# Prompt attention moved between the value steps of layer 1, and four dot rows moved ahead of the query tiles

## The reference, cut to what matters

```python
qp, kp, vp = _qkv(hp, na_w_qkv[j], na_b_qkv[j])          # prompt: 128 tokens
op = _merge_heads(_context_attention(qp, kp, vp)) @ na_w_out[j] + na_b_out[j]
new_k_layers.append(kp); new_v_layers.append(vp)
qs, ks_, vs = _qkv(hs, na_w_qkv[j], na_b_qkv[j])         # sample: 256 tokens
att = _neighbourhood_attention(qs, ks_, vs, cache_k[:, j], cache_v[:, j], na_rpb[j])
os_ = _merge_heads(att) @ na_w_out[j] + na_b_out[j]
yp = _layer_norm(DEEPNORM_ALPHA * yp + gm_p * op, ln_g[i, 0], ln_b[i, 0])
```

## Time and profile before

| | |
|---|---|
| median of three executions | 1055.6 us |
| the profiled execution's own time | 1054.8 us |
| its span from first to last instruction | 1053.0 us |
| busy: PE, DVE, ACT, POOL | 983.7, 704.7, 184.1, 196.6 us |
| mean granted clock of PE | 0.970 |
| chain that ended last: PE, DVE, DMA, SP's queue | 72%, 9%, 9%, 6% |

### The profile page before, as it was taken

The page is one execution under the profiler, slowest core; times in us unless marked ns, Lnnn a source line. Parts: engine busy times, 40 slices in busy tenths (PEclk is TensorE's granted clock), DMA queues, the critical chain, the costliest instruction groups (busy, mean ns, idle before and its releaser), DMA issues.

```text
span 1053.0 us, 28184 instructions
## 1 busy us (share of the span) xinstructions
PE 983.7 (93%) x11412; PEld 585.2 (56%) x11412; DVE 704.7 (67%) x1782; ACT 184.1 (17%) x435; POOL 196.6 (19%) x304
## 2 busy tenths in 40 slices
PE   7999999999899999999899999899979999999872
PEld 2555555565556656566545554575445666666451
DVE  6458874955756666666667995685576666666457
ACT  4342223003210000000140010562231000000002
POOL 1400000610132222222110000354013222222112
PEclk9999999999899999999999999799989999999896
DMA  9964666950999999999996788532088899999991
GB/s 332 401 246 164 235 249 224 390 165 18 354 343 406 405 405 405 406 405 405 395 390 214 271 323 331 188 93 79 0 325 312 345 405 405 405 405 406 406 373 60
DMA packets 102208, 318.29 MB, mean 302 GB/s; under 512 B 8403, under 2 KB 12691, under 8 KB 101748
## 3 DMA queue, kind: packets, MB, share of 16 engines
q1 hardware_dynamic: 92228, 298.87, 73.8%
q0 software_dynamic: 5776, 17.30, 4.8%
q10 hardware_dynamic: 4128, 1.05, 0.4%
HBM read 311.44 MB, written 5.77 MB: 301 GB/s over the span
## 4 chain that ended last, share of the span: by engine, by line
PE 72%; DVE 9%; DMA 9%; SPq 6%; POOL 2%; issue 2%; ACT 1%; DVEq 0%; ACTq 0%; POOLq 0%
PE bank L794 69%; SPq L513 5%; DMA ring<-in_moe_w_down 4%; DMA ring<-in_na_w_qkv 1%; DMA group_row<-token_rows,rows_now 1%; DMA row_beta<-in_ln_b 1%; POOL P L768 1%; PE bank L1269 1%; DVE P L2111 1%; DVE x L1833 1%; PE bank L1009 1%; DVE tmp L1832 0%; DVE st L2045 0%; DVE st L1843 0%; DVE x L1842 0%
## 5 line engine op out<-in xcount | busy, mean ns | idle before, releaser
L794 PE MATMUL bank<-ring,xgT 128*32 128x256 f32 x4224 | 245.4, 383 | 7.8 <-DMA ring<-in_moe_w_up 4.9
L794 PE MATMUL bank<-hT,ring 128*128 128x384 f32 x640 | 207.2, 486 | 0.1
L794 PEld LDWEIGHTS bank<-ring,xgT 128*32 128x32 f32 x4224 | 147.7, 110 | 87.1 <-issue 8.3
L794 PEld LDWEIGHTS bank<-hT,ring 128*128 128x128 f32 x640 | 121.4, 190 | 85.9 <-issue 2.1
L1624 DVE CUSTOM_DVE_ANT_0 ring<-ring,ring 128x1024 f32<-128x1024 f32 x112 | 137.0, 1224 | 3.5
L794 PE MATMUL bank<-ring,heT 128*32 128x256 f32 x2112 | 129.4, 382 | 5.5 <-DMA ring<-in_moe_w_down 5.2
L794 PEld LDWEIGHTS bank<-ring,heT 128*32 128x32 f32 x2112 | 62.9, 109 | 56.5 <-DVE heT L2004 15.4
L1481 ACT ACTIVATE sa<-bank 128x128 f32<-128x128 f32 x66 | 18.3, 278 | 426.7 <-PE bank L794 426.7
L2002 DVE TENSOR_TENSOR he<-sa,bank 128x128 f32<-128x128 f32 x66 | 19.0, 288 | 100.2 <-ACT sa L1481 100.2
L794 PE MATMUL bank<-y,ohT 32*128 32x256 bf16 x2448 | 80.3, 271 | 4.8 <-DVE y L2031 4.6
L734 POOL DMA_INDIRECT group_row<-token_rows,rows_now x68 | 74.4, 1094 | 17.4 <-issue 17.1
(11 more groups left out here) (296 smaller groups left out, 1176.2 us busy)
## 6 DMA issues: line engine op xcount, KB each, us to landing
ring<-in_moe_w_up SPq DMA_DIRECT2D x64, 2048.0 KB
ring<-in_moe_w_down SPq DMA_DIRECT2D x32, 2048.0 KB
ring<-in_k_ada SPq DMA_DIRECT2D x14, 2048.0 KB
ring<-in_w_ada SPq DMA_DIRECT2D x10, 2048.0 KB
ring<-in_na_w_qkv SPq DMA_DIRECT2D x6, 2048.0 KB
ring<-in_hy_w_in SPq DMA_DIRECT2D x5, 2048.0 KB
ring<-in_hy_w_out SPq DMA_DIRECT2D x2, 2048.0 KB
ring<-in_na_w_out SPq DMA_DIRECT2D x2, 2048.0 KB
```

Source lines behind the costliest of these rows:

```text
L794: return nc.tensor.matmul(out, lhsT, rhs, start=first, stop=last)
```

## The change: what it does

Three things move, and what they touch in PSUM and SBUF is laid out anew.

- The prompt's eight units go between the 24 value steps of `v_10` to `v_12`, three steps to a unit: PE does `scores(n)` and `weigh(n-2)`, a value step, `flip(n-1)`, two value steps. The new keys and the gate rows stand behind the last value step, around the scores of unit 8. ACT and DVE get the matching orders.
- Two of the four dot rows of the first piece go ahead of `values(0, 2)`, two behind it; behind each block of queries stand two rows as before, which now are rows 4 to 19.
- SP loads the first three biases ahead of expert piece 0 and the others ahead of piece 4.

For this the prompt's scores use banks 0 and 1 for every unit (they alternated over 0 to 3), both its heads are transposed into bank 4 and copied by ACT in one instruction, its probabilities have a tile of their own (`Pp`), the gate rows are copied by ACT instead of DVE, `bv` lies elsewhere, and the values' second half, new keys and gate rows take turns on banks 2, 3 and 5.

```diff
+SIDE_AT, SIDE_END, SIDE_BANKS = G_AT["v_10"], G_AT["out1_00"], (2, 3, 5)
...
                     if i == RING + EXTRA:
                         sp.wait_ge(nb_ready, l + 1)
+                    if l == 1 and i == 0:
+                        load_biases(range(3))
                     if l == 1 and i == 4:
-                        load_biases()
+                        load_biases(range(3, 2 * PAIRS))
...
             wait_weights(pe, W_AT["qkv_5"])
-            for t in range(TT):
-                bank(G_AT[f"v_1{t}"])
-                value_steps(1, t, range(KT))
-            wait_all_evacuated(pe, G_AT["v_10"])
...
             def scores(u):
                 t, j = divmod(u, PAIRS)
-                if u >= 2:
-                    pe.wait_ge(p_ready if u - 2 < PAIRS else max_ready, 2 * (u - 1))
-                S = [ps[2 * (u % 2) + i] for i in range(2)]
+                if u == 0:
+                    for g in range(SIDE_AT - 8, SIDE_AT - 4):
+                        wait_evacuated(pe, g)
+                elif u <= PAIRS:
+                    pe.wait_ge(p_ready, 2 * u)
+                elif u >= PAIRS + 2:
+                    pe.wait_ge(max_ready, 2 * (u - 1))
+                if 4 <= u < PAIRS:
+                    wait_evacuated(pe, SIDE_AT - 8 + u)
+                if u == PAIRS:
+                    pe.wait_ge(att_in, 32)
+                if u == PAIRS + 1:
+                    wait_evacuated(pe, G_AT["gm1a"] + 1)
+                    wait_evacuated(pe, G_AT["gm1b"])
+                S = [ps[2 * (u % 2) + i] if t > 0 else ps[i] for i in range(2)]
...
-            for n in range(units + 3):
+            for s in range(TT * KT):
+                t, k = divmod(s, KT)
+                n, part = divmod(s, 3)
+                if part == 0:
+                    scores(n)
+                    if n >= 2:
+                        weigh(n - 2)
+                elif part == 1 and n >= 1:
+                    flip(n - 1)
+                if k == 0:
+                    bank(G_AT[f"v_1{t}"])
+                value_steps(1, t, (k,))
+            weigh(PAIRS - 2)
+            new_keys()
+            flip(PAIRS - 1)
+            scores(PAIRS)
+            pe.wait_ge(mod_ready, 6)
+            gates("gm1a", 1, 16, (0,))
+            weigh(PAIRS - 1)
+            gates("gm1b", 1, 16, (1,))
+
+            for n in range(PAIRS + 1, units + 3):
                 if n < units:
                     scores(n)
...
+            for n in range(PAIRS):
+                exponentials(n)
+                if n >= 1:
+                    turned(n - 1)
+                if n == 4:
+                    values_out()
+            turned(PAIRS - 1)
+            keys_out()
+            gates_copied("gm1a", 0)
+            exponentials(PAIRS)
+            wait_evacuated(act, G_AT["v_12"])
+            gates_copied("gm1b", 1)
...
-            for t in range(TT):
-                values(0, t)
+            values(0, 0)
+            values(0, 1)
+            dot_row(1, 0)
+            dot_row(1, 1)
+            values(0, 2)
+            dot_row(1, 2)
+            dot_row(1, 3)
...
-                for r in (2 * j, 2 * j + 1):
+                for r in (2 * j + 4, 2 * j + 5):
                     dot_row(1, r)
...
+            for n in range(PAIRS):
+                maximum(n)
+                reciprocals(n)
+                if n in (2, 5, 7):
+                    values(1, n // 3)
+                if n == 5:
+                    heads_out(0)
+            maximum(PAIRS)
+            reciprocals(PAIRS)
+            heads_out(1)
```

More of the change, by code:

```diff
@@ L497, in load, with load_biases @@
                              ).then_inc(w_loaded[W_SLOT[i]], 16)
-            def load_biases():
+            def load_biases(which):
                 sp.wait_ge(ln_done, TT * 2)
                 sp.wait_ge(rows_landed, 1)
-                for m in range(2 * PAIRS):
+                for m in which:
                     if m >= 3:
@@ L790, in bank @@
                     wait_evacuated(pe, g - 8)
+                if SIDE_AT + 3 <= g < SIDE_END:
+                    wait_evacuated(pe, g - 3)
+                elif SIDE_AT <= g < SIDE_END:
+                    for before in range(SIDE_AT - 8, SIDE_AT):
+                        if bank_of(before) == bank_of(g):
+                            wait_evacuated(pe, before)
                 return ps[bank_of(g)]
@@ L1224, in _, with new_keys @@
             wait_weights(pe, W_AT["qkv_5"])
-            for t in range(TT):
-                bank(G_AT[f"v_1{t}"])
-                value_steps(1, t, range(KT))
-            wait_all_evacuated(pe, G_AT["v_10"])
[L1230 to L1239, removed]
+            def new_keys():
+                for h in range(2):
+                    out = bank(G_AT["kctx"] + h)
+                    for j in range(4):
+                        last = nc.tensor.transpose(out[:, j * 128:(j + 1) * 128], kT[:, 4 * h + j, 0:128], ident[:])
+                    last.then_inc(group_ready, 1)
             units = TT * PAIRS
@@ L1262, in flip @@
                 pe.wait_ge(scaled[1], u + 1)
+                if u == 0:
+                    wait_evacuated(pe, SIDE_AT - 2)
+                if u == PAIRS:
+                    wait_all_evacuated(pe, SIDE_END)
                 if u >= 1:
                     pe.wait_ge(pt_ready[0], u)
-                    pe.wait_ge(pt_ready[1], u)
+                if u > PAIRS:
+                    pe.wait_ge(pt_ready[1], u - PAIRS)
                 for i in range(2):
-                    for c in range(1 if u < PAIRS else 3):
+                    if u < PAIRS:
+                        last = nc.tensor.transpose(ps[4][:, i * 128:(i + 1) * 128], Pp[:, u % 3, i, :], ident[:])
+                    for c in range(0 if u < PAIRS else 3):
                         cs = slice(c * 128, (c + 1) * 128)
@@ L2083, in _ @@
                                 ALU.add, ALU.mult).then_inc(evacuated[g % 8], 1)
-                for r in (2 * j, 2 * j + 1):
+                for r in (2 * j + 4, 2 * j + 5):
                     dot_row(1, r)
-            for r in range(2 * KT, DOT_ROWS[1]):
+            for r in range(2 * KT + 4, DOT_ROWS[1]):
                 dot_row(1, r)
@@ L2089, in _ @@
             v.memset(credit[:, 4:5], 0.0).then_inc(mod_ready, 1)
[L2090 to L2096, removed]
             units = TT * PAIRS
@@ L2133, in heads_out @@
                               ps[6 + w % 2][:, :].rearrange("p (j n) -> p j n", j=4)).then_inc(o_evac, 1)
-            for n in range(units + 4):
+            for n in range(PAIRS):
[8 more added lines that the diff above has]
+            heads_out(1)
+            for n in range(PAIRS + 1, units + 4):
                 if n < units:
                     maximum(n)
-                if 0 <= n - 1 < units:
+                if PAIRS < n - 1 < units:
                     reciprocals(n - 1)
-                if 0 <= n - 2 < units:
+                if PAIRS <= n - 2 < units:
                     turned(n - 2)
-                if n >= 4 and n % 4 == 3:
+                if n >= 12 and n % 4 == 3:
                     heads_out(n // 4 - 1)
```

69 lines of the change are left out of this document (42 added, 27 removed).

## The result

The change took 1048.62 us, median of five executions (1047.83 to 1049.24); the kernel before, measured beside it, 1056.12 (1055.33 to 1061.93). The ratio is 0.9904, with an interval of 0.9885 to 0.9923: faster by about 1%. The profiled execution of the change took 1049.24 us, its span 1047.4.

The account below looks back on a forecast made before the run. PE was taken as the bound, with the prompt's units at half clock. Dots early, a 29.1 us loop and 6.5 us behind it bring unit 9's flip 7.1 us sooner: 1054.8 - 7.1 = 1047.7 us, range 1045.5 to 1052.5.

Parts of the forecast that it names:

- The dots: DVE's dot rows, ahead of the prompt's units: done at about 635.6 us in place of 645.08, weights landing in time.
- The loop: 24 value steps with the prompt's jobs between: 29.1 us from 635.9 to 665.0, rounds of 3.6, no wait.
- The clock in the loop: Clock at 1.00 through the value steps; rival of a cold loop, 13.2 us lost, 1060.9 us, 6%.
- Behind the loop: Weighing, new keys, unit 8 and gate rows: 6.5 us on PE; unit 9's scores wait for the third gate copy.
- Unit 9's flip: In attention behind the loop: starts at 676.6 to 677.3 in place of 683.88, taken as 7.1 us sooner.
- The biases: SP's queue: three 256 KB biases ahead of expert piece 0, under 2.5 us; unmoved, they land behind expert piece 3.
- What follows: From unit 9's flip on nothing changes; attention's end and expert piece 4 move by the same 7.1 us.
- The rivals: Clock falling behind the loop 11%, cold loop 6%, late dots (1055) 3%, later stage giving part back (1050 to 1053) 6%.
- Where the clock fell in the kernel before: Ahead of the prompt's units: the clock fell in PE's 0.98 us wait for DVE's gate copies.
- rival of a clock that falls behind the loop: PE's waits around scores 9 to 11: 6.3 us lost to a cold stretch, about 1054 us; 11%, shorter falls included.
- What bounds the kernel: PE in layer 1; the prompt's units run at half speed, 1.97 us each against 1.08 at full clock.

Follow-up runs that it names:

- run 1: The change with its dot rows put back behind the blocks of queries, as in the kernel before: 1058.54 us, ratio to before 1.0004.
- run 2: The kernel before with only the four dot rows moved ahead: 1058.27 us, ratio to before 1.0001.
- Run 5: The change with half the second pair of gate rows behind unit 8's flip, DVE copying one prompt gate row: 1048.04 us, ratio to before 0.9907.
- Run 4: The change with all biases loaded ahead of expert piece 4, as before: 1056.56 us, ratio to before 0.9991.
- Run 3: The kernel before with three unread 128x512 matmuls in PE's waits, behind the gate rows and unit 1's scores: 1053.14 us, ratio to before 0.9955.

## Why the prediction was right, step by step

The forecast was 1047.7 us, the measured median is 1048.62 and the profiled execution 1049.24. The mechanism came as told: dots done in time, a loop without a wait, full clock. That the time is so near is in part luck. Of the 1.5 us between forecast and profile, 2.4 are the late start; against it stand 0.7 in the load of `row_beta` and 0.4 behind unit 9's flip. None of the three stood in a step of the sum.

- **The dots** were to end 0.3 us ahead of the loop; they end 0.4 ahead, with no wait for weights. (The slack of those weights, put at about 2 us, is 3.2 by the prediction's own numbers: 615.8 and 5.4 against 624.4.) That they had to is shown by run 1 (7.01 us of wait, 7.7 worked out), that the move costs and gains nothing alone by run 2.
- **The loop** was to take 29.1 us without a wait, with rounds of 3.6: it takes 29.32 with rounds of 3.78 and no wait. By the round's rows, six value matmuls take 2.77 us where I had 2.60 and scores 0.42 where I had 0.37, while transposes take 0.22 in place of 0.34. So a change of job into a step costs some 0.09 us and not the 0.05 that I took. Over the loop, changes and scores were too cheap by about 1.0 us together and transposes too dear by 0.8: the total is right because two errors cancel.
- **The clock in the loop** was granted at 1.00 from 638.31 to 667.63, with PE busy all the time. The Trainium skill (TensorE: Matmul & The Clock Gate, "A second HAM failure mode: psum-queue depth-cycling") describes a clock that swings between its levels when PE stops briefly between groups of matmuls on changing banks. This loop changes banks with every job but PE doesn't stop in it, in either profile of the change, so it doesn't put that rule to the test; changing banks alone didn't bring the clock down.
- **Behind the loop** scores 9 were to start 6.65 us after it, and do so after 6.97. PE is busy 6.87 of the 6.97 us. Its last gate row ends at 674.49 and ACT's third gate copy at 674.45, so which of them held the scores is not shown; the sum had both within 0.1 us of each other too. Run 5, which moves a quarter of the gate rows into a wait, takes 1.0 us off attention.
- **Unit 9's flip** was to come 7.1 us sooner and comes 7.01 sooner, counted from the loop start. Here too errors cancel: the loop is 0.2 us longer than forecast and the scores behind it 0.3 later, while from scores to flip it is 4.69 us where 7.1 implied 5.1. From the flip to the end of attention nothing was to change; it is 38.55 us in place of 38.96, and what the 0.4 are stays open.
- **The biases** had no price in the sum but a reason: without the move they land behind piece 3. Run 4 gives the price of leaving them, 7.0 us of attention, not far from the 8.7 of leaving the dots (run 1). The prediction gave it one sentence.
- **What follows** was to shift by the same amount: from the end of attention to piece 4 it is 0.68 us shorter, all of it in the load of `row_beta`, and behind piece 4 the same.
- **The rivals**: no clock fell behind the loop or in it, no dot was late, and no later stage gave anything back. That a wait of PE behind the loop could bring the clock down was a fair worry: in run 4 and run 1, where PE waits 6 to 7 us, it does fall; in the change, where it waits 1.46 us ahead of unit 9's flip, it doesn't. The Trainium skill (TensorE: Matmul & The Clock Gate, "HAM oscillation — how this bites in real kernels") says that a wait for a DMA is followed by matmuls at the half clock; run 4's scores, 1.22 us in place of 0.70 behind a wait that a late bias began, agree.
- **Where the clock fell in the kernel before** was misread. I had it fall in the wait of 0.98 us ahead of the prompt's units. Two stretches of the first profile of before, and PE's rows at their border:

```profile
662.08:664.30 2.22, 1.20 (x12) 0.82 (x12) 1.33 (x6) 1.37 (x8) 0.25 (x1) 1.00 1.04 411
664.80:678.10 13.30, 13.30 (x66) 7.52 (x66) 7.61 (x35) 6.34 (x31) 4.18 (x6) 0.50 0.38 114
```

```profile
663.79 0.49 PE L794 MATMUL bank<-kT,qT 64*128 64x128 f32 x4 [1.00 <-ACT P L1553]
664.80 0.69 PE L1269 MATMUL bank<-first,P 128*128 128x128 f32 x2 [0.51 <-POOL P L768]
```

The scores of units 0 to 2 still ran at 1.00. The clock fell two waits later, in the one of 0.51 us behind one of 1.00, both for the chain of the first units through DVE, ACT and POOL, and stayed at 0.50 for 13.3 us. This doesn't touch the price of the cold stretch, but the reason given for the rival of a clock that falls behind the loop.

- **What bounds the kernel** was told too simply. I read a unit's 1.97 us as jobs at half clock that would take 1.08 at full clock. Run 3 shows that full clock alone gives 1.43, because the chain through POOL comes next. Against the first profile of before, the clock is 3.4 us of the gain; the other 4.1 I put down to covering the chain with value steps, but no run takes the new places of the gate copies and the one copy per unit apart from that. The sum came out right since in the loop both happen at once.

The measured difference of medians, 7.5 us in the first comparison and 8.3 in the last, is more than the 5.6 between the first two profiles. Late starts are in either kernel; the executions of the kernel before run from 1053.88 to 1063.14 us, and that of its first profile, 1054.8, is near the lowest; and the cold stretch of the kernel before can be longer than in the profile that I used (88.32 us of attention in place of 86.95). That this explains the medians is argued from two profiles of each kernel, not shown on every execution.

## What to carry to other kernels

When an engine's many small jobs run slowly, ask two questions apart: at which clock, and what is the chain of the other engines at full clock; three useless matmuls in the waits answer the first for a few lines of code. Putting the jobs between long independent matmuls settled both here, but only because everything that the first job needs (here the dot rows, some 90 us upstream) and that the first job behind the loop needs (three biases in a DMA queue) was moved up too: undoing either of them gave back all, or nearly all, of the gain. And read two profiles of the kernel before: a stretch whose clock differs between them may be time to win, and it makes one profile a poor yardstick for a microsecond.

## What had not been expected of the hardware

The same program, on the same data, was granted different clocks in two places from one execution to the next: 0.69 or 0.53 over 22 us of the prompt's units, and 0.93, 0.86 or 0.79 over the 24 us from 516 on, which went with a shift of all that follows by some 2.5 us. For the second place the chip is not the reason, since all three values occur on each of two chips; for the first this isn't shown. Three matmuls that do nothing, 3.0 us of work by their rows, placed in waits, made the kernel before 0.45% faster. And 256 KB issued 0.5 us behind a 2 MB piece on one queue were usable 9.8 us later.
